# Moving an output product, norms and turns between two blocks of a recurrent kernel

## The reference

```python
    S, y = lax.scan(step, S0, ...)                       # recurrence, 16 heads of 64
    mean = jnp.mean(y, axis=-1, keepdims=True)
    var = jnp.mean(jnp.square(y - mean), axis=-1, keepdims=True)
    y = (y - mean) * lax.rsqrt(var + RW_GN_EPS)
    y = y * gn_w + gn_b
    y = y + jnp.sum(r_h * k_h * r_k, axis=-1, keepdims=True) * v_h
    x = x + (y * g) @ w_out                              # first block's output
    xn = _rms_norm(x, norm_g) * (1.0 + sc_x) + sh_x      # second block
    cn = _rms_norm(ctx, norm_g) * (1.0 + sc_c) + sh_c
    ... xn @ w_in, cn @ w_in
```

## Time and profile before

| | us |
|---|---|
| median of 3 runs | 823.29 |
| lowest and highest run | 821.58, 829.12 |
| profiled execution, its own time | 819.92 |
| span in the profile | 818.0 |
| PE busy | 762.1 (93%) |
| DVE, ACT, POOL busy | 446.0, 306.6, 172.3 |

### The profile page before, as it was taken

How to read it: one execution, slowest core, us unless ns; L and a number is a source line. 1 busy time by engine, 2 the same in 40 slices (tenths; PEclk the granted TensorE clock), 3 DMA queues, 4 the chain that set the end, 5 groups by cost and what they waited for, 6 DMA issues and landing times.

```text
span 818.0 us, 17638 instructions
## 1 busy us (share of the span) xinstructions
PE 762.1 (93%) x7612; PEld 618.4 (76%) x7612; DVE 446.0 (55%) x800; ACT 306.6 (37%) x638; POOL 172.3 (21%) x133
## 2 busy tenths in 40 slices
PE   3999999999998998988859899999999999999997
PEld 3588887777786787877847788877777777775697
DVE  5944635777879233556544123749655666754611
ACT  5534445566531122334331235523225453424200
POOL 2334330000342212324210000740000000002642
PEclk9999999999999599999978899999999999999999
DMA  7133233224458663310031134213302111231131
GB/s 245 30 100 103 78 100 107 78 79 91 123 126 217 141 220 125 128 55 4 4 121 35 52 103 112 62 53 92 113 3 76 52 53 53 62 107 52 51 105 52
DMA packets 116765, 72.83 MB, mean 89 GB/s; under 512 B 26832, under 2 KB 114128, under 8 KB 116688
## 3 DMA queue, kind: packets, MB, share of 16 engines
q1 hardware_dynamic: 98496, 65.12, 27.0%
q10 hardware_dynamic: 18192, 6.58, 3.3%
HBM read 64.35 MB, written 7.34 MB: 88 GB/s over the span
## 4 chain that ended last, share of the span: by engine, by line
PE 83%; DVE 9%; issue 3%; ACT 2%; DMA 2%; POOLq 0%; POOL 0%; SPq 0%; ACTq 0%; DVEq 0%
PE bank L524 21%; PE bank L983 9%; PE bank L518 6%; PE bank L520 6%; PE bank L519 6%; PE bank L647 2%; PE bank L1024 2%; PE bank L1007 2%; DVE arena L1613 2%; PE bank L780 2%; PE bank L696 2%; PE bank L543 2%; PE bank L679 2%; PE bank L1103 2%; PE bank L1105 2%
## 5 line engine op out<-in xcount | busy, mean ns | idle before, releaser
L524 PE MATMUL bank<-arena 128*128 128x256 f32 (+1 forms) x768 | 182.6, 396 | 4.5 <-DVE arena L1715 3.1
L524 PEld LDWEIGHTS bank<-arena 128*128 128x128 f32 x768 | 147.1, 194 | 38.4 <-issue 16.0
L1979 POOL TENSOR_TENSOR w_lo<-arena,w_hi 128x1024 fp32r<-128x1024 f32 x24 | 58.1, 2419 | 179.7 <-ACT w_hi L1196 179.7
L1196 ACT ACTIVATE w_hi<-arena 128x1024 fp32r<-128x1024 f32 x44 | 46.4, 1057 | 86.3 <-DMA arena<-w_in 84.6
L518 PE MATMUL bank<-x_hi,w_hi 128*128 128x512 f32 x192 | 76.4, 398 | 0.0
L520 PE MATMUL bank<-x_hi,w_lo 128*128 128x512 f32 x192 | 75.6, 394 | 0.0
L519 PE MATMUL bank<-x_lo,w_hi 128*128 128x512 f32 x192 | 75.3, 392 | 0.0
L518 PEld LDWEIGHTS bank<-x_hi,w_hi 128*128 128x128 f32 x192 | 36.1, 188 | 8.7 <-issue 0.8
L520 PEld LDWEIGHTS bank<-x_hi,w_lo 128*128 128x128 f32 x192 | 36.0, 188 | 8.4
L2076 POOL COPY arena<-arena 128x512 f32<-128x512 f32 x4 | 2.5, 614 | 189.2 <-DVE arena L1889 189.2
L519 PEld LDWEIGHTS bank<-x_lo,w_hi 128*128 128x128 f32 x192 | 36.1, 188 | 8.0
(11 more groups left out here) (252 smaller groups left out, 1636.6 us busy)
## 6 DMA issues: line engine op xcount, KB each, us to landing
arena<-w_in SPq DMA_DIRECT2D x45, 512.0 KB, 3.9
arena<-w_ada SPq DMA_DIRECT2D x12, 1024.0 KB, 5.1
arena<-w_in SPq DMA_DIRECT2D x8, 1024.0 KB, 5.4
arena<-w_out SPq DMA_DIRECT2D x8, 1024.0 KB, 5.1
lt_dram<-arena ACTq DMA_DIRECT2D x16, 256.0 KB, 2.3
arena<-x SPq DMA_DIRECT2D x4, 512.0 KB, 5.6
arena<-x SPq DMA_DIRECT2D x1, 2048.0 KB, 7.6
out<-arena SPq DMA_DIRECT2D x8, 256.0 KB, 2.1
```

The costliest lines, as they stand in the source:

```text
L524: last = mm(o, lhs(k), rhs(k), start=(k == 0), stop=(k == n - 1))
L1196: A(WHI[n % 3][:, :], WR[n % 3][:, 0:1024], ACT.Copy).then_inc(weights_rounded, 1)
L1979: TT(WLO[n % 3][:, :], WR[n % 3][:, 0:1024], WHI[n % 3][:, :].bitcast(f32), SUB)\
```

## The change

project_y now makes 256 columns (a half of what it made), named by a third number i; both halves go to one bank, and the second one counts it full. All weights are taken at its first call. Three halves are moved into the last turns of the loop: (0,0,0) at g = 15 and (0,0,1) at g = 16, behind from_state, and (0,1,0) at g = 17, ahead of scan_out. Tile 2 is turned behind the loop, and then come (1,0,0), (1,0,1), (1,1,0) and (2,0) ahead of tile 3's turns, and (0,1,1), (1,1,1) and (3,0) behind them. On the second block's side both turns of x1's tiles 0 and 1 stand behind (2,1). The banks of the outputs and of the turns of tiles 2 and 3 are given by numbers (6, 7 and others instead of the next of six), and the count of next_bank starts again at 0. DVE divides tile 1 and 2 (norm_y) ahead of finish_y of the tile before; the norm of tile 3 is interleaved with the taking of tile 2 on ACT and DVE. ACT squares the context before it takes tile 3. DVE makes x1 of tiles 0 and 1 in full, and norms them, before it adds the last parts of tiles 2 and 3. SP issues ctx without waiting for the gating. The loop ends at g = 17 on PE and ACT and at 16 on DVE.

```diff
@@ -799,7 +799,7 @@
                     pe.wait_ge(y_normed, j + 1)
                     pe.wait_ge(bv_ready, j + 1)
                 name, src = ("yT", YT[j]) if piece % 2 == 0 else ("bT", V[:, j, :])
-                o = out_bank((name, j, h), 3) if j < NT - 1 else next_bank((name, j, h))
+                o = out_bank((name, j, h), 3 if j < 2 else ((3, 0, 1, 2), (1, 2, 7, 4))[j - 2][piece])
                 ov = o.rearrange("p (a k e t) -> p a k e t", a=2, k=2, e=2)
                 for a in range(2):
                     for e in range(2):
@@ -823,8 +823,26 @@
             for b in range(8):
                 if b not in (4, 5, MODS_BANK) and uses[b]:
                     pe.wait_ge(bank_free[b], uses[b])
+            wo = []
+            OUT_BANKS = {(0, 0): 4, (0, 1): 5, (1, 0): 6, (1, 1): 3, (2, 0): 0, (3, 0): 6}
+
+            def project_y(t, h, i):
+
+                pe.wait_ge(y_gated, 2 * (t + 1))
+                if not wo:
+                    wo.extend([weights() for _ in range(3)] + [WX])
+                if (h, i) == (1, 1):
+                    pe.wait_ge(wx_here, 16)
+                if i == 0:
+                    out_bank(("o", t, h), OUT_BANKS[t, h]) if (t, h) in OUT_BANKS else next_bank(("o", t, h))
+                b = where["o", t, h][0]
+                last = accumulate(banks[b][:, i * 256:(i + 1) * 256], lambda k: YG[t][:, k, :],
+                                  lambda k: wo[2 * h + i][:, k, :])
+                if i:
+                    last.then_inc(bank_full[b], 1)
+
             pe.wait_ge(y_zeroed, 1)
-            for g in range(-1, GROUPS + 5):
+            for g in range(-1, GROUPS + 2):
                 now, nxt, old = 0 <= g < GROUPS, g + 1 < GROUPS, 0 < g <= GROUPS
                 if nxt:
                     off_product(g + 1, 0)
@@ -833,10 +851,14 @@
                         rhs_values(g - 1, i)
                 if now:
                     off_product(g, 1)
+                if g == GROUPS + 1:
+                    project_y(0, 1, 0)
                 if 0 <= g - 2 < GROUPS:
                     scan_out(g - 2)
                 if old:
                     from_state(g - 1)
+                if g in (GROUPS - 1, GROUPS):
+                    project_y(0, 0, g - GROUPS + 1)
                 if nxt:
                     turned(g + 1)
                 if g >= 0:
@@ -853,23 +875,6 @@
                 mods_here(g, 2)
                 if 9 <= g < 17:
                     turn_y((g - 1) // 4 - 2, (g - 1) % 4)
-                if g == 17:
-                    for piece in range(4):
-                        turn_y(2, piece)
-
-
-            wo = [weights(), weights()]
-
-            def project_y(t, h):
-                pe.wait_ge(y_gated, 2 * (t + 1))
-                if (t, h) == (0, 1):
-                    wo.extend([weights(), WX])
-                    pe.wait_ge(wx_here, 16)
-                o = next_bank(("o", t, h))
-                for i in range(2):
-                    last = accumulate(o[:, i * 256:(i + 1) * 256], lambda k: YG[t][:, k, :],
-                                      lambda k: wo[2 * h + i][:, k, :])
-                last.then_inc(bank_full[where["o", t, h][0]], 1)
 
             def turn_x1(t):
                 pe.wait_ge(xn_ready, t + 1)
@@ -880,13 +885,16 @@
                                                    ident)
                     last.then_inc(bank_full[where["xT", t, h][0]], 1)
 
-            for t in range(3):
-                project_y(t, 0)
+            for piece in range(4):
+                turn_y(2, piece)
+            for t, h, i in ((1, 0, 0), (1, 0, 1), (1, 1, 0), (2, 0, 0), (2, 0, 1)):
+                project_y(t, h, i)
             for piece in range(4):
                 turn_y(3, piece)
-            project_y(3, 0)
-            block_key[taken[0] - 2] = block_key[taken[0] - 1] = ("o", 3, 0)
-            project_y(0, 1)
+            for t, h, i in ((0, 1, 1), (1, 1, 1), (3, 0, 0), (3, 0, 1)):
+                project_y(t, h, i)
+            block_key[taken[0] - 3] = block_key[taken[0] - 2] = ("o", 3, 0)
+            turn[0] = 0
             pe.wait_ge(cn_ready, 2)
             for h in range(4):
                 o = next_bank(("cT", h))
@@ -927,12 +935,13 @@
                 if len(items) > 1:
                     head_norm(len(items) - 2)
 
-            project_y(1, 1)
-            project_y(2, 1)
+            for i in range(2):
+                project_y(2, 1, i)
             turn_x1(0)
-            project_y(3, 1)
+            turn_x1(1)
+            for i in range(2):
+                project_y(3, 1, i)
             block_key[taken[0] - 1] = ("o", 3, 1)
-            turn_x1(1)
             for h in range(4):
                 stored(pe, ("cT", h))
             for nb in range(2):
@@ -1141,7 +1150,6 @@
                     sp.wait_ge(y_made, GROUPS)
                     sp.dma_start(XR, x_t).then_inc(x_again, 16)
                     sp.dma_start(WX, cols(w_out, 768, 256)[0]).then_inc(wx_here, 16)
-                    sp.wait_ge(y_gated, 2 * NT)
                     sp.dma_start(CX, ctx_x.rearrange("(t p) n -> p t n", p=P)).then_inc(ctx_here, 16)
                 if n == 46:
                     sp.dma_start(NEAR, near).then_inc(rel_here, 16)
@@ -1342,6 +1350,17 @@
                     act.wait_ge(mods_block, n + 1)
                     A(MROW, banks[MODS_BANK][:, 0:256], ACT.Copy).then_inc(mods_copied, 1)
 
+            def square_y(j):
+                act.wait_ge(centred, j + 1)
+                if j:
+                    act.wait_ge(gn_sums, j)
+                A(SQ, YT[j], ACT.Square).then_inc(gn_squared, 1)
+
+            def root_y(j):
+                act.wait_ge(gn_sums, j + 1)
+                A(GST[:, 128 + 16 * j:144 + 16 * j], GST[:, 64 + 16 * j:80 + 16 * j], ACT.Sqrt, bias=gn_eps,
+                  scale=1.0 / HD).then_inc(gn_root, 1)
+
             def take_y(j, h):
 
                 o = arrived(act, ("yT", j, h))
@@ -1366,22 +1385,16 @@
                 copy_mods(g, 2)
                 if 9 <= g < 17 and g % 2 == 1:
                     take_y((g - 1) // 4 - 2, (g - 1) % 4 // 2)
-                if g == 17:
-                    take_y(2, 0)
-                    take_y(2, 1)
                 j = (g - 1) // 4 - 1
-                if g >= 6 and g % 4 == 2:
-                    act.wait_ge(centred, j + 1)
-                    if j:
-                        act.wait_ge(gn_sums, j)
-                    A(SQ, YT[j], ACT.Square).then_inc(gn_squared, 1)
-                if g >= 7 and g % 4 == 3:
-                    act.wait_ge(gn_sums, j + 1)
-                    A(GST[:, 128 + 16 * j:144 + 16 * j], GST[:, 64 + 16 * j:80 + 16 * j], ACT.Sqrt, bias=gn_eps,
-                      scale=1.0 / HD).then_inc(gn_root, 1)
-
-            take_y(3, 0)
-            take_y(3, 1)
+                if 6 <= g < GROUPS and g % 4 == 2:
+                    square_y(j)
+                if 7 <= g < GROUPS and g % 4 == 3:
+                    root_y(j)
+
+            square_y(3)
+            take_y(2, 0)
+            root_y(3)
+            take_y(2, 1)
             act.wait_ge(ctx_here, 16)
             for t in range(2):
                 own.own(A(CNJ, CX[:, t, :], ACT.Square, accum_out=SUMS[:, t:t + 1]))
@@ -1404,8 +1417,11 @@
                                 bias=MODS[:, c, 0:1], scale=GSC[:, c, 0:1])
                     free(ins, ("xT", t, h))
 
+            take_y(3, 0)
+            take_y(3, 1)
             act.wait_ge(mods_ready, 1)
             square_x1(0)
+            square_x1(1)
             for h in range(4):
                 o = arrived(act, ("cT", h))
                 for i in range(2):
@@ -1413,11 +1429,10 @@
                     ins = A(CNT[:, c, :], o[:, i * 256:(i + 1) * 256], ACT.Identity, bias=MODS[:, c, 1:2],
                             scale=GSC[:, c, 1:2])
                 free(ins, ("cT", h))
-            square_x1(1)
             square_x1(2)
             take_x1(0)
+            take_x1(1)
             square_x1(3)
-            take_x1(1)
 
             def root(i):
                 n = CTX if ITEMS[i][0] == "ck" else T
@@ -1727,7 +1742,16 @@
             stat = lambda i, j: GST[:, 64 * i + 16 * j:64 * i + 16 * j + 16]
             bc = lambda a: a.unsqueeze(2).broadcast_to([P, HEADS, HD])
             heads_of = lambda a: a.rearrange("p (h n) -> p h n", n=HD)
-            for g in range(-1, GROUPS + 5):
+            def sum_y(j):
+                dve.wait_ge(gn_squared, j + 1)
+                nc.vector.tensor_reduce(stat(1, j), heads_of(SQ), AX.X, ADD).then_inc(gn_sums, 1)
+
+            def norm_y(j):
+                dve.wait_ge(gn_root, j + 1)
+                own.own(nc.vector.reciprocal(stat(2, j), stat(2, j)))
+                TT(heads_of(YT[j]), heads_of(YT[j]), bc(stat(2, j)), MUL).then_inc(y_normed, 1)
+
+            for g in range(-1, GROUPS + 1):
                 now, nxt, old = 0 <= g < GROUPS, g + 1 < GROUPS, 0 < g <= GROUPS
                 if nxt:
                     mask_z(g + 1, 0)
@@ -1744,22 +1768,21 @@
```

(37 more changed lines are left out.)

## The result

| | us |
|---|---|
| median of 4 runs of the changed kernel | 800.51 (798.41 to 802.61) |
| median of 4 runs of the kernel before, beside them | 822.43 (821.36 to 829.12) |
| ratio | 0.9756, 95% interval 0.9715 to 0.9798 |
| profiled execution, own time and span | 801.25 and 799.4 |

A forecast was written before the change was run, and what follows sets the result against it. PE in order, with holes in its queue and low clock behind them, bounds the stretch; 91.93 us less 68.6 of work gives 23.3, less 0.2 for (i) and (e): 23.1, so 823.29 becomes 800.2 us, 8 in 10 within 796 to 807.5.

The forecast's parts named there:

- the stretch: From turn 15's L726 to the first product of the context keys: 91.93 us before, 68.6 of work at full clock.
- (a) to (c): Turns 15 to 17: the three halves cover PE's waits; the last scan_out ends at 425.6, 4.0 us later.
- (d): Tile 2's norm ahead of finish_y(1, 1), at about 417 to 419: its four turns wait for nothing, 425.6 to 427.4.
- (e): PE before (2,0,0): tile 2's gating chain 11.7 us, PE's cover 12.1, margin 0.4; reduction beside GpSimd's multiply costs 0.
- (f): Before (3,0): two halves cover tile 3's gating, ready by 450; the 3.13 us wait and its low clock go.
- (g): Loads behind the last scan_out: ctx no longer waits for the gating, lands near 439, is squared before tile 3's banks.
- (h) and (j): x1's norms done near 458, wanted at 469, first context product 477.6 to 478; later banks cost 0, at most 1.4 us.
- (i): Turn 12: the norm ahead of finish_y puts DVE's masks about 0.6 us later, costing 0 to 0.5 us.
- a late gate of tile 2: Chain before (2,0,0) 2 us or more longer: 2.3 + 3.24 = 5.5 us back, 805.7 us; chance 0.16 with its like.
- The second rival: Behind the changed part, something running by its own time makes PE wait, half to all lost: 812 to 823 us; chance 0.03.
- The slower rival: From 410 us, halves mixed with 64x64 matmuls bring the clock down and it stays: 868 us; chance 0.02.
- It doesn't do what it says: Halves in the turns merely put off the chain by 4 us, another hole stays: 807 us; counted with the first rival.

The follow-up runs named there:

- the kernel with the old orders: Changed kernel's PE order and banks, but the old order of divisions and tile 3's norm on DVE and ACT, ctx after the gating: 800.15 us, ratio 0.9735.
- the halves alone: Kernel before with only the three halves moved into the turns, outputs and tile 3's turns given banks by number: 815.27 us, ratio 0.9910.
- the fills behind: Changed kernel with halves (0,1,1) and (1,1,1) behind (3,0) instead of ahead of it: 810.87 us, ratio 0.9853.
- three reductions more: Changed kernel with three unused 128x1024 reductions added on DVE in the chain of tile 2's gating: 806.39 us, ratio 0.9809.
- the four banks: Changed kernel with all four pieces of tile 2's turns through bank 3 instead of four banks: 808.09 us.
- the kernel with the halves behind: Changed kernel with halves (0,0,0), (0,0,1), (0,1,0) behind the loop, ahead of tile 2's turns: 809.35 us, ratio 0.9832.

## Why the prediction was right

**The bound** was read rightly: PE in order, holes in its queue, and the clock behind them. Without the holes the stretch is PE's work at full clock, 68.8 us against 68.6.

**(a) to (c)** hold. All three halves run without a wait, and grow and scan_sa behind them too. The last scan_out ends at 428.9, 16.8 us behind L726's start; 425.6 was forecast for a start at 409.38, 16.2 us behind it. The 0.6 us are the size of what the sum had set aside for groups that stand alone, and had not placed.

**The waits before the turns.** The prediction puts the 7.4 us of the earlier trace rows before the turns of tiles 2 and 3. All of it stood before those of tile 2; tile 3's followed at 455.00 without a wait. The sum isn't touched by that.

**(d)** The four turns of tile 2 wait for nothing, as forecast, but for another reason: the halves put them off past the norm's end in either order. I gave the order of the norm a part in the gain; by the kernel with the old orders it has none.

**(e)** The critical place was the right one, and its margin was mis-sized only a little: 0.4 us forecast, 0.6 to 0.7 measured. The open price, the reduction beside GpSimd's multiply, is read from DVE's and GpSimd's timelines of the changed kernel:

```profile
429.40 1.22 DVE L1719 TENSOR_REDUCE arena<-arena 128x16 f32<-128x1024 f32 x1 [3.01 <-ACT arena L1345]
430.65 0.38 DVE L1720 TENSOR_SCALAR arena<-arena 128x16 f32<-128x16 f32 x1
431.06 1.22 DVE L1721 TENSOR_TENSOR arena<-arena 128x1024 f32<-128x1024 f32 x1
...
439.84 0.69 DVE L1730 SCALAR_TENSOR_TENSOR arena<-arena 128x512 f32<-128x512 f32 x1
```

```profile
429.10 1.91 POOL L2055 TENSOR_TENSOR arena<-arena 128x1024 f32<-128x1024 f32 x1 [15.87 <-PE bank L760]
```

GpSimd multiplies from 429.10 to 431.01 and the reduction lies wholly beside it, at 1.22 us; the sum of the same shape, L1747 at 436.14 with GpSimd idle, took 1.21. The value taken, 0, was right. The centring's multiply starts at 431.06, when GpSimd has ended, and takes 1.22 us. The division, which took 2.64 us beside GpSimd, is at 420.45 now with GpSimd idle, and takes 1.23. (This is as the Trainium skill has it, "GPSIMD Engine Reference", section Specifications: contention for VectorE instructions with two SBUF inputs. The reduction has one, and no slowing is seen.) What I did not see is that the interleaving alone makes this place critical: with the old order of the norms its margin is near 7 us.

**(f)** holds. The hole of 3.13 us is gone; put back by one line, it returns with its clock and with a second hole of 2.31 us before the context turns, so the edit is worth 10.5 us in the changed kernel, where the prediction had 3.13 + 3.24 = 6.4 for the hole: the sum over the stretch held, the share of this part was too small.

**(g)** ACT starts on ctx at 442.51, 13.6 us behind the last scan_out's end, as forecast (439 less 425.6 is 13.4). It changes nothing in the time.

**(h) and (j)** The turns of x1 and the context products wait for nothing. The longest wait behind is 1.4 us as before. **(i)** can't be told from nothing: from L726 of turn 12 to that of turn 15 the changed kernel took 22.1 and 22.7 us in its two profiles, the kernel before 22.1 and 21.5, and the one with the old orders 22.7.

**The rivals.** The first, a late gate of tile 2, didn't occur, but was near: with 1.24 us more in the chain PE waits. Its price was too high. I took the clock behind a hole as a fixed 3.24 us, from one row, and 0.16 of it came from setting 17.06 us of the timeline against 13.82 of the chain, which leaves out the overlap with the next row. In the timeline 64 records at full clock are 13.98 us. By that the runs gave 3.1 and 1.8 us behind the very same hole of 3.13 us in two executions of the kernel before, 3.1 with the halves alone, 3.0 with the fills behind, and 1.7 behind 3.15 us with three reductions more. The second rival, a gain eaten further on, didn't occur either: the part behind is 316.9 and 318.6 us in the two profiles of the kernel before, and 316.8 to 318.6 in those of the new order, by the clock in that one product. The slower rival, products at the low level, didn't occur: 332 matmuls, products mixed with 64x64 ones, were granted 1.00. "It doesn't do what it says" fell with the windows.

**The parts don't add up.** Taken out of the changed kernel one at a time, the halves cost 4.9 us, the four banks 12.0, the fills 10.5: 27.4 of 23.1. Put into the kernel before, the halves alone bring some 10 us (90.96 or 91.77 to 81.26). What one part takes away is also what another part needs: with the halves in the turns the norm's wait is gone, and with the norm interleaved the one bank waits twice as long.

**The number.** That 800.2 came within 0.3 us is partly luck. The 23.1 us of the stretch are met to the tenth, but the medians are only 21.9 us apart. The kernel before had a median of 822.43 us beside the changed one, not 823.29, and the same kernel gave 801.75 when it was run again. What lies outside the stretch moves single executions by several us either way.

**What stays open.** What the low clock costs behind a hole follows from how long it stays: in the first profile of the kernel before it is 0.50 from 460 to 466 us and 0.98 or more from there, so half of 6 us is lost; in the second it is 0.50 for 3.4 us (466.60 to 470.01) and 1.00 from 470, which is 1.7 us. Why it stays longer in one execution than in another, behind the same hole and in the recurrence, no run here tells.

## What to carry to other kernels

Where one engine works in order and has independent work left, sum that work at full clock; if the stretch is longer than the sum, look at each wait and put a piece of that independent work of the wait's length ahead of it, cut in halves if need be. Before other engines' queues are reordered to shorten a chain, ask whether the filled-in work has not covered it already: here the reordering brought nothing and used up nearly all of a margin of 7 us. Compare two kernels by the stretch that the change touches, not by two spans: outside it the same instructions took up to 11 us more or less.

## What the runs showed of the hardware

A hole of PE can cost more than its length, and not by a fixed sum: 3.13 or 3.15 us of waiting were followed by 1.7, 1.8, 3.0, 3.1 and 3.1 us of loss at the low clock in five profiles; 1.42 us by 0 or 1.7. A wait of 0.64 us cost no clock: the 32 records behind it took 7.17 us, where 32 at full clock show 7.07.

In the recurrence the granted clock between 260 and 300 us was 0.57 in one execution and 0.96 in another of the same order of instructions, with PE busy 33.5 and 31.7 us of 40. The start of the stretch moved by up to 11 us with it, more than the 9 us by which single runs of the changed kernel differ (798.41 to 807.43).

VectorE's reduction beside GpSimd's multiply of the same size kept its 1.22 us (1.21 in the kernel with the halves behind), while VectorE's own multiply beside it had gone from 1.23 to 2.64 us, in both profiles of the kernel before: 1.41 us more for 1.56 us that the two lay side by side.
